# Attention blocks of a two-layer encoder: twelve copies per layer move from ScalarE to VectorE

## The chip, the cores and the metric

One core of a Trainium2 chip runs the whole program. The time is the device time of one execution, in microseconds (us), as a median of several runs. Engines are named as the profile names them: PE is TensorE, DVE is VectorE, ACT is ScalarE, POOL is GpSimd.

## The reference

Two layers, each of them (1024 tokens, width 1024):

```python
h = rms_norm(x, attn_norm[l])
x = x + hybrid_mixer(h, w_in[l], qk_gain[l], rpb[l], sink[l], out_gain[l], w_out[l])
h = rms_norm(x, ffn_norm[l])
x = x + swiglu(h, w_gu[l], w_down[l])
```

The mixer has three head groups that read the same normalised input: A, neighbourhood attention on a grid (4 heads); B, windowed attention with a sink (6 query heads on 2 key/value heads); C, dilated attention with three branches (6 heads). For every head and query block it computes

```python
p = exp(scores + bias - max)
o = (p @ v) / sum(p)
```

The head groups are normalised, joined and multiplied by `w_out`. The change touches only how `p` reaches the product `p @ v`.

## The kernel before

Each layer first makes values, queries and keys (long runs of matmuls), then does the attention, then the output projection and the feed-forward part. The attention is written out by hand as steps `k = 0` to 57 over 224 tiles, four tiles a step. A tile is one head of one block of 128 queries; its scores are 128 x 128 to 128 x 384. Steps 0 to 23 are the dilated branches. From step 24 on there are eight blocks of 128 queries with 16 tiles each, so four steps a block: tiles 0 to 3 of a block are group B (`TB` is the bias table), 4 and 5 are B too, 6 to 11 are C (`TC`), 12 to 15 are A (`TA`).

In step `k` the engines do, each in its own fixed order:

- PE (`pe_step`): the scores of the step's first pair of tiles (L2414; they wait for all four `tmin` of the step before), the scores of its second pair (they wait for the copies of the first group of the step before), the products `p @ v` of the tiles of step `k-2` (`weigh`, L2524; they wait for the copies made in step `k-1`), and then the transposes of the probabilities of step `k-1` (`half_units`, L2480).
- DVE (`dve_step`): four times `tmin` (L1682: bias table plus scores from PSUM into `T`, and the row's minimum), between them small pieces of the block's end (`finish`: denominators at L1744 to L1753, `own_heads` at L1759, `squares` at L1714, `mean` at L1720), then this engine's copies of turned probabilities (`copy_unit`, L1856), then the last piece, `finish(k, 4)`; in the first step of a block that is `own_heads`.
- ACT (`act_step`): four exponentials (L1244, each waits for its `tmin`), a result copy (L1237), one copy of turned probabilities after the third exponential, and its other copies (L1266, L1261) after the fourth.
- POOL: the weighted sum of the three branches of group C: three products (L2276, `G<-G,fac_c`) and two sums (L2288), then powers and scalings (L2234, L2241).

The turned probabilities of a step lie in one or two groups, each of them two PSUM banks: queries 0 to 63 of every chunk (first half) in one bank, queries 64 to 127 (second half) in the other. Each bank is copied by one instruction into a slot of `PT` in SBUF. A second group is there when four tiles have 12 chunks of 128 keys; then both groups hold six chunks and the copies are 128 x 384. This is so in steps 29, 32, 33, 36, 37, 40, 41, 44, 45, 48, 49 and 52, in both layers: the first step (`k` a multiple of 4) of the five blocks that begin at steps 32 to 48 and of the one at 52, and the second step (29 to 49) of six blocks. A second group of only two chunks is copied by one instruction, and its engine is as before.

Which engine makes a copy is set in one line by the copy's place `i` in the step (0 and 1 are the halves of the first group, 2 and 3 those of the second):

```python
u["engine"] = (0 if len(pt_rows) == 1 or k <= 12 or i == 1 else 1)
```

Engine 0 is DVE, 1 is ACT.

Of the kernel before, what the change touches and what calls it, by code (L numbers as in the profile page):

```python
# [22 lines left out]
def build_program(nc, x, gains, w_in, rpb, w_out, w_gu, w_down, out):  # L23
# [43 lines left out]
    with ctx:  # L67
# [241 lines left out]
        for l in range(depth):  # L309
          with ExitStack() as layer:  # L310
# [145 lines left out]
            def chunks_of(bd, s):  # L456

                k = bd["kind"]
                if k == "c3":
                    return [0]  # L460
                if k == "c2" or k in ("b0", "b7") or 6 <= s < 12:
                    return [0, 128]
                return [0, 128, 256]
# [16 lines left out]
            def first_group(b):  # L480

                return 24 + 4 * b
# [9 lines left out]
            def y_halves(fam, n, b, pair_, off):  # L492

                return dict(y=(fam, 0, n, b), items=[], engine=1, pair=pair_, off=off, half="both", group=1)
# [20 lines left out]
            def turn_of(k):  # L515

                return k if k > DILATED_STEPS else 0
# [12 lines left out]
            def by_halves(k):  # L530

                return k >= 3

            for k in range(1, GROUPS + 1):
                rows = steps[k]
                for n in range(4 * k - 4, 4 * k):
                    need = len(chunks_of(*tiles[n]))
                    if by_halves(k):
                        if not rows or len(rows[-1]["items"]) + need > 8:
                            group = len(rows) // 2  # L540
                            pair_ = TRIO[(turn_of(k) + 2) % 3] if not group else TRIO[k % 3]
                            for half in range(2):
                                rows.append(dict(y=None, items=[], engine=None, bank=pair_[half], slot=n_pt % 4, half=half,
                                                 group=group, pair=pair_))
                                n_pt += 1
                        for c in chunks_of(*tiles[n]):
                            place_of[n, c] = (rows[-2], rows[-1], len(rows[-1]["items"]))
                            for u in rows[-2:]:
                                u["items"].append((n, c))
                        continue  # L550
                    if not rows or len(rows[-1]["items"]) + need > 4:
                        pair_ = TRIO[(turn_of(k) + 2) % 3] if len(rows) < 2 else TRIO[k % 3]
                        i = max(k - 2, 0) % 2 if need == 1 else len(rows) % 2
                        rows.append(dict(y=None, items=[], engine=None, bank=pair_[i], slot=n_pt % 4, half=None, group=0))
                        n_pt += 1
                    for c in chunks_of(*tiles[n]):
                        place_of[n, c] = (rows[-1], rows[-1], len(rows[-1]["items"]))
                        rows[-1]["items"].append((n, c))
                for fam, after in (("b", 6), ("a", 7), ("c", 7)):
                    b, left = divmod(k - after - first_group(0), 4)  # L560
                    if left == 0 and 0 <= b < MT - 1:
                        used = max((u["off"] + 64 * FAM[u["y"][0]][1] if u["y"] else 64 * len(u["items"])
                                    for u in rows if u["group"]), default=0)
                        rows.append(y_halves(fam, FAM[fam][1], b, TRIO[k % 3], used))
                assert len(rows) <= 5
                second = [u for u in rows if u["group"] and u["y"] is None]
                if second and len(second[0]["items"]) <= 4:
                    first_, both_ = second
                    rows.remove(first_)
                    n_pt -= 1  # L570
                    both_.update(half="both", slot=first_["slot"])
                    for n, c in both_["items"]:
                        place_of[n, c] = (both_, both_, place_of[n, c][2])
                pt_rows = [u for u in rows if u["y"] is None]
                for i, u in enumerate(pt_rows):
                    u["engine"] = (0 if len(pt_rows) == 1 or k <= 12 or i == 1 else 1)
                order += rows
            Y_TAIL = [y_unit("b", 0, 2, MT - 1, 0, 6), y_unit("b", 2, 1, MT - 1, 1, 7), y_unit("c", 0, 3, MT - 1, 0, 6),
                      y_unit("a", 0, 2, MT - 1, 1, 7)]
# [2193 lines left out]
```

## Time and profile before

| | |
|---|---|
| median of 3 runs | 2332.53 us (2332.25 to 2333.1) |
| profiled execution, its own time | 2333.02 us |
| span of its core | 2331.3 us |
| mean granted TensorE clock | 0.998 |
| PE busy | 2280.3 us, 98% |
| DVE busy | 1617.7 us, 69% |
| ACT busy | 1056.9 us, 45% |
| POOL busy | 662.2 us, 28% |

Busy shares are means over stages with different limits. The attention blocks take about 322 to 434 us and 1480 to 1597 us of the span.

### The profile page before, as it was taken

The page shows a single profiled execution, that of the slowest core. Times are in us where ns is not written, and L with a number is a line of the kernel's source. Part 1 is how long each engine was busy: PE and PEld are TensorE (multiplying, and loading weights), DVE is VectorE, ACT ScalarE, POOL GpSimd, SP SyncE. Part 2 cuts the span into 40 slices and gives each one's busy share as a digit, 9 for nine tenths or more (in the row PEclk, how much of TensorE's full clock was granted, in tenths as well). Part 3 has the DMA queues.
Part 4 walks back from the last instruction along what each step waited for, and adds up shares of the span by engine and source line. Part 5 has one row for each costly group of instructions (what it writes and reads, how often), then busy time and mean ns, then how long its engine had stood idle before and what let it go on. Part 6 is the DMA issues. An engine that isn't in the chain of part 4 may idle for free. (4 is left out here: it accounts for less than half of the span.)

```text
span 2331.3 us, 40658 instructions
## 1 busy us (share of the span) xinstructions
PE 2280.3 (98%) x15508; PEld 1885.0 (81%) x15508; DVE 1617.7 (69%) x2921; ACT 1056.9 (45%) x2022; POOL 662.2 (28%) x571
## 2 busy tenths in 40 slices
PE   9999999999999999999999999999999999999999
PEld 9988776787888888888898887667878888888887
DVE  5389989748555555789844999896475555557898
ACT  4333689645222222443533337895452222224434
POOL 1000466312444444100010005562124444440000
PEclk9999999999999999999999999999999999999999
DMA  7231341332222211821352213313322222218223
GB/s 248 65 54 54 82 132 33 124 109 73 82 82 82 82 55 55 313 66 68 118 176 58 55 45 107 107 39 121 104 73 82 82 83 88 60 42 316 69 81 104
DMA packets 234285, 225.35 MB, mean 97 GB/s; under 512 B 50548, under 2 KB 192372, under 8 KB 234104
## 3 DMA queue, kind: packets, MB, share of 16 engines
q1 hardware_dynamic: 234104, 222.90, 30.2%
q8 instruction: 119, 1.95, 0.4%
q14 instruction: 62, 0.51, 0.1%
HBM read 171.00 MB, written 53.41 MB: 96 GB/s over the span
## 5 line engine op out<-in xcount | busy, mean ns | idle before, releaser
L1962 DVE TENSOR_TENSOR WL<-RAW,WH 128x512 fp32r<-128x512 f32 x132 | 160.4, 1216 | 151.4 <-ACT WH L1396 151.4
L2718 PE MATMUL psum<-ABH 128*128 128x512 f32 x616 | 240.1, 390 | 1.1 <-DVE X L2045 1.1
L2720 PE MATMUL psum<-ABH,ABL 128*128 128x512 f32 x616 | 239.7, 389 | 0.0
L2719 PE MATMUL psum<-ABL,ABH 128*128 128x512 f32 x616 | 239.7, 389 | 0.0
L2684 PE MATMUL psum<-HL,WH 128*128 128x512 f32 x704 | 217.4, 390 | 0.7 <-DVE HL L1968 0.7
L2684 PE MATMUL psum<-OPH_t,WH 128*128 128x512 f32 x528 | 206.0, 390 | 3.5 <-DVE U L1983 3.5
L2684 PE MATMUL psum<-OPL_t,WH 128*128 128x512 f32 x528 | 205.7, 390 | 1.0 <-DVE OPH_t L1968 1.0
L1962 DVE TENSOR_TENSOR WL<-WS,WH 128x512 fp32r<-128x512 f32 x172 | 138.4, 806 | 84.2 <-ACT WH L1396 84.2
L2316 POOL TENSOR_TENSOR WS<-RAW 128x512 f32<-128x512 f32 x84 | 143.3, 1706 | 132.0 <-DMA x_res<-X 132.0
L2348 PE MATMUL psum<-HH,UH 128*128 128x512 f32 x448 | 174.5, 389 | 0.0
L2350 PE MATMUL psum<-HH,UL 128*128 128x512 f32 x448 | 174.4, 389 | 0.0
L2349 PE MATMUL psum<-HL,UH 128*128 128x512 f32 x448 | 174.3, 389 | 0.0
L1634 DVE RECIPROCAL RM<-RM 128x512 f32<-128x512 f32 x52 | 174.0, 3346 | 0.0
L2684 PEld LDWEIGHTS psum<-HL,WH 128*128 128x128 f32 x704 | 131.7, 188 | 29.1 <-DVE HL L1968 1.5
L2209 POOL COPY QS<-QK 128x384 f32<-128x384 f32 x32 | 30.9, 965 | 435.5 <-DVE QK L1637 253.9
L2348 PE MATMUL psum<-PH,HH 128*128 128x512 f32 (+1 forms) x384 | 143.8, 374 | 0.0
L2350 PE MATMUL psum<-PH,HL 128*128 128x512 f32 (+1 forms) x384 | 142.6, 371 | 0.0
L2349 PE MATMUL psum<-PL,HH 128*128 128x512 f32 (+1 forms) x384 | 142.4, 371 | 0.0
L1244 ACT ACTIVATE T<-T,G 128x192 f32<-128x192 f32 (+3 forms) x304 | 132.1, 477 | 22.0 <-DVE G L1682 21.1
L2684 PE MATMUL psum<-OPH_b,WH 128*128 128x512 f32 x352 | 137.4, 390 | 0.0
L2718 PEld LDWEIGHTS psum<-ABH 128*128 128x128 f32 x616 | 115.6, 188 | 26.6 <-DVE X L2045 2.0
L2684 PE MATMUL psum<-OPH_t,WL 128*128 128x512 f32 x352 | 137.0, 389 | 0.0
(276 smaller groups left out, 5546.7 us busy)
## 6 DMA issues: line engine op xcount, KB each, us to landing
RAW<-in_w_gu SPq DMA_DIRECT2D x176, 256.0 KB, 3.9
WDS<-in_w_down SPq DMA_DIRECT2D x88, 256.0 KB, 2.6
UR<-in_w_in SPq DMA_DIRECT2D x56, 256.0 KB, 3.4
g_mid<-GRES SPq DMA_DIRECT2D x28, 512.0 KB, 2.6
WDK<-in_w_down SPq DMA_DIRECT2D x44, 256.0 KB, 6.3
x_res<-X SPq DMA_DIRECT2D x2, 4096.0 KB, 13.4
PR<-in_w_out SPq DMA_DIRECT2D x32, 256.0 KB, 5.1
X<-x_res SPq DMA_DIRECT2D x2, 4096.0 KB, 13.5
```

Source lines behind the costliest of these rows:

```text
L1244: a.activation(T[:, t_slot(n), off:off + w], T[:, t_slot(n), off:off + w], ACT.Exp, scale=-1.0, bias=G[:, 6 * V1 + place_:6 * V1 + place_ ...
L1634: v.reciprocal(RM[:, hf, :], RM[:, hf, :]).then_inc(rec_s, 1)
L1962: v.tensor_tensor(WL[SLOT[i, j]][:, :, :], w_source(i, j), WH[SLOT[i, j]][:, :, :].bitcast(F32), ALU.subtract).then_inc(w_lo, 1)
L2209: g.tensor_copy(dst, dilated_rows(bd, T_CQ, q, P)).then_inc(staged, 1)
L2316: g.tensor_tensor(to[i][:, :, :], first, second, op).then_inc(w_sum, 1)
L2348: t.matmul(dst, sh, mh, start=start, stop=False)
L2349: t.matmul(dst, sh, ml, start=False, stop=False)
L2350: return t.matmul(dst, sl, mh, start=False, stop=stop)
L2684: last = t.matmul(dst[:, :], w[SLOT[i, j]][:, k, :], h[o][:, k, :], start=(i in (1, 5, 6) and k == 0 and part == 0), stop=(i in (2, 3, 4) ...
L2718: t.matmul(dst, ah, bh, start=open_, stop=False, skip_group_check=True)
L2719: t.matmul(dst, ah, bl, start=False, stop=False, skip_group_check=True)
L2720: last = t.matmul(dst, al, bh, start=False, stop=shut, skip_group_check=True)
```

## The change

In steps after 12 the copies with an odd place go to DVE: 1 as before and now 3 too. So the second half of the second group goes from the end of ACT's step to DVE, right behind DVE's copy of the first group's second half and ahead of `finish(k, 4)`. PE's waits follow the engine of each copy.

```diff
                 for i, u in enumerate(pt_rows):
-                    u["engine"] = (0 if len(pt_rows) == 1 or k <= 12 or i == 1 else 1)
+                    u["engine"] = (0 if len(pt_rows) == 1 or k <= 12 or i % 2 else 1)
```

## Rows read from the trace of the kernel before

**Rows 1.** The page: span, and busy us (share) of each engine.

```profile
span 2331.3 us, 40658 instructions
PE 2280.3 (98%) x15508; PEld 1885.0 (81%) x15508; DVE 1617.7 (69%) x2921; ACT 1056.9 (45%) x2022; POOL 662.2 (28%) x571
```

**Rows 2.** Windows of two blocks: length, busy PE, PEld, DVE, ACT, POOL, clock, DMA.

```profile
354.08:370.02 15.94, 15.28 (x302) 11.07 (x303) 14.98 (x62) 14.63 (x36) 10.29 (x11) 1.00 0.14 41
370.02:385.94 15.92, 15.10 (x302) 10.99 (x300) 14.96 (x63) 14.54 (x35) 10.28 (x11) 1.00 0.14 42
```

**Rows 3.** Groups by form, 320 to 450 us: copies of 128 x 384 on either engine.

```profile
L1856 DVE COPY PT<-psum 128x384 f32<-128x384 f32 x12 | 6.6, 550 | 0.3 <-PE psum L2480 0.3
...
L1266 ACT ACTIVATE PT<-psum 128x384 f32<-128x384 f32 x36 | 16.1, 485 | 0.0
```

**Rows 4.** Waits, 320 to 430 us: total us, times, longest.

```profile
ACT T L1244 <- DVE GB L1682: 5.3, 10, 0.8
...
DVE T L1682 <- PE psum L2414: 2.8, 8, 0.4
```

**Rows 5.** Timeline of DVE, steps 40 and 41: start, us.

```profile
372.21 0.69 DVE L1753 TENSOR_TENSOR coef<-den,fac_b 128x6 f32<-128x6 f32 x1
372.83 0.54 DVE L1856 COPY PT<-psum 128x384 f32<-128x384 f32 x1
373.30 0.80 DVE L1759 TENSOR_TENSOR Y<-GB,coef 128x384 f32<-128x384 f32 x1
374.02 0.54 DVE L1682 CUSTOM_DVE_ANT_0 T<-TB,psum 128x384 f32<-128x384 f32 x1
...
374.49 0.72 DVE L1714 CUSTOM_DVE_ANT_0 junk<-Y 128x384 f32<-128x384 f32 x1
...
375.14 0.54 DVE L1682 CUSTOM_DVE_ANT_0 T<-TB,psum 128x384 f32<-128x384 f32 x1
...
376.36 0.56 DVE L1856 COPY PT<-psum 128x384 f32<-128x384 f32 x1
...
377.27 0.42 DVE L1682 CUSTOM_DVE_ANT_0 T<-TC,psum 128x256 f32<-128x256 f32 x1 [0.35 <-PE psum L2414]
```

**Rows 6.** Timeline of POOL in the same steps (windows overlap).

```profile
372.05 0.84 POOL L2276 TENSOR_TENSOR G<-G,fac_c 128x390 f32<-128x390 f32 x1 [3.60 <-ACT fac_c L1254]
...
372.85 1.95 POOL L2276 TENSOR_TENSOR G<-G,fac_c 128x390 f32<-128x390 f32 x2
...
373.64 1.15 POOL L2276 TENSOR_TENSOR G<-G,fac_c 128x390 f32<-128x390 f32 x1
...
374.87 1.22 POOL L2288 TENSOR_TENSOR G<-G 128x390 f32<-128x390 f32 x1
...
376.17 1.01 POOL L2288 TENSOR_TENSOR G<-G 128x390 f32<-128x390 f32 x1
```

**Rows 7.** Timeline of PE, steps 40 to 43, in two windows.

```profile
371.57 0.97 PE L2480 MATMUL psum<-ident,T 64*128 64x64 f32 x24
...
376.51 0.69 PE L2414 MATMUL psum<-QK 64*128 64x256 f32 x4
...
365.86 0.92 PE L2414 MATMUL psum<-QK 64*128 64x384 f32 x4 [0.32 <-DVE PT L1856]
```

**Rows 8.** Timeline of ACT, steps 40 and 41.

```profile
373.63 0.86 ACT L1266 ACTIVATE PT<-psum 128x384 f32<-128x384 f32 x2
374.60 0.62 ACT L1244 ACTIVATE T<-T,GB 128x384 f32<-128x384 f32 x1
375.73 0.62 ACT L1244 ACTIVATE T<-T,GB 128x384 f32<-128x384 f32 x1 [0.51 <-DVE GB L1682]
```

**Rows 9.** Timeline of DVE and POOL, steps 52 and 53.

```profile
421.09 0.55 DVE L1759 TENSOR_TENSOR Y<-GB,coef 128x384 f32<-128x384 f32 x1
...
421.12 2.32 POOL L2276 TENSOR_TENSOR G<-G,fac_c 128x390 f32<-128x390 f32 x2
...
421.56 0.41 DVE L1682 CUSTOM_DVE_ANT_0 T<-TB,psum 128x256 f32<-128x256 f32 x1
...
424.34 0.69 DVE L1856 COPY PT<-psum 128x512 f32<-128x512 f32 x1 [0.63 <-PE psum L2480]
```

## The prediction, as put on record before the kernel ran

> **What bounds the kernel now.** I read the page first. PE is busy 98% of the span and DVE only 69% [rows 1], which would make a longer DVE program harmless; but these are means over stages, and the change lies in one stage. So I cut that stage into its blocks with the windows view. A block of four steps takes 15.9 us, of which PE is busy 15.1 to 15.3, DVE 15.0 and ACT 14.5 to 14.6 [rows 2]. All three look full, so the busy shares can't choose between them, and I asked the view of waits and the timeline which one is late. Within a block ACT's exponentials stand idle for `tmin` on DVE: 5.3 us in 10 waits for the B tiles alone [rows 4]. In the steps that change, the first exponential of step 41 starts at 374.60, just behind its `tmin`, and the next comes 0.51 us late for the same reason [rows 5, 8]. PE in turn starts the second pair of scores of a block's last step on DVE's copy [rows 7]. DVE itself waits for PE in few places; in the two steps that matter here it does once, 0.35 us ahead of 377.27, for scores (2.8 us in 8 such waits over seven blocks [rows 4]). So DVE's own order of instructions sets the pace through the first two steps of a block, and what is added there is paid unless it falls into that one gap.
>
> **What is removed.** Twelve copies a layer, 24 in all, leave ACT. A copy takes 0.485 us [rows 3], but two in a row take 0.86 us together [rows 8], so one gives back 0.86 - 0.49 = 0.37 us. It stood behind the step's last exponential. The next thing on ACT is the exponential of the next step, and that waits for DVE [rows 8]: at a block's first step ACT only waits 0.37 us longer. At a block's second step ACT's following exponentials do come earlier, but PE's next scores there wait for DVE's copy [rows 7]. I value the removal at nothing. Its cover is DVE's lateness; if that were gone, it would be worth 24 x 0.37 = 8.9 us.
>
> **What is added, second step of a block (29 to 49).** DVE gets a copy of 128 x 384, 0.55 us as a row [rows 3]; from its start to the next instruction's it is 373.30 - 372.83 = 0.47 us [rows 5]. It goes in at the gap. From the copy at 376.36 to the next `tmin` at 377.27 there are 0.91 us, because PE can begin the scores only after the fourth `tmin` (its row starts at 376.51 [rows 7]). Two copies take 0.94 to 0.96. So I charge 0.05 us, six times a layer. From below it is 0.03; from above it is the full 0.47, if the copy has to wait for the second group's transposes, which run just ahead of those scores.
>
> **What is added, first step of a block (32 to 48).** Here there is no gap. DVE runs copy 372.83, `own_heads` (L1759) 373.30, `tmin` 374.02 [rows 5]. The second group's transposes are done at about 371.57 + 0.97 = 372.54 [rows 7], so the new copy doesn't wait. It starts at 373.30 and sends `own_heads` to 373.77. Simply added, that is 0.47 us.
>
> But L1759 takes 0.80 us here and 0.55 at step 52 [rows 5, 9], and L1753, six elements wide, takes 0.69 and ends with POOL's first product (372.05 + 0.84 = 372.89, at 372.83 DVE goes on) [rows 5, 6]. Both read two operands from SBUF, as POOL's products do. L1759's extra 0.25 fits a wait until 373.55, which is 0.70 after POOL's second product began at 372.85. In return POOL's third product takes 1.15 instead of 0.84: the two engines take turns, a whole instruction each. So *when* `own_heads` arrives matters, and the copy moves it past a turn:
>
> 1. POOL's third product starts at 373.64 [rows 6], now ahead of `own_heads` (373.77). It runs alone, 0.84, and lets go after 0.70, at 374.34.
> 2. `own_heads` runs 374.34 to 374.89; the next `tmin` starts 0.08 before that end, as it does now (373.30 + 0.80 = 374.10 against 374.02), at 374.81. It stood at 374.02: 0.79 late.
> 3. `squares` (L1714) is issued 0.47 later, at 375.28. POOL's first sum (L2288) can't start before `own_heads` lets go at 374.81; alone it takes 1.01 [rows 6], so it ends at 375.82 and lets go 0.14 earlier (0.84 - 0.70), at 375.68.
> 4. `squares` runs 0.55 from there (0.72 today, with 0.17 of waiting), and the next `tmin` starts at 375.68 + 0.55 - 0.08 = 376.15. It stood at 375.14: 1.01 late.
>
> After that DVE has no instruction with two SBUF operands until the next step. I charge 1.0 us, five times a layer. The bounds: 0.05 if the added copy fills the time in which `own_heads` and `squares` wait for POOL today (0.47 - 0.25 - 0.17); 1.0 from above, by the steps just listed.
>
 By that rule the added copy costs more than its own length here, 1.0 us a block as against 0.47 simply added; the rows above agree with it, and the sum doesn't need it.
>
> **What is added, step 52.** Here POOL runs 0.4 us later against DVE: `own_heads` starts at 421.09, just ahead of POOL's second product at 421.12 [rows 9]. With the copy in front it comes at 421.56, waits until 421.12 + 0.70 = 421.82, and the next `tmin` starts at 421.82 + 0.55 - 0.08 = 422.29 instead of 421.56: 0.73 late. Step 53 ends with 0.63 us of idle time in front of DVE's copy, where DVE waits for PE [rows 9]; PE's work there doesn't depend on these `tmin`. That leaves 0.10.
>
> **What moves.** The waits in front of PE's products and transposes now name DVE's copy instead of ACT's last one. In step 40 ACT's last copy ends at 373.63 + 0.86 = 374.49, DVE's new one at about 373.85: earlier, but nobody waited for it. No DMA, no instruction of PE or POOL is added.
>
> **The sum.** Per layer 5 x 1.0 + 6 x 0.05 + 0.10 = 5.4 us; two layers 10.8 us. Delays of one block are not made good in the next, since PE's last step of a block starts on DVE's copy [rows 7]. The profiled execution's own time is 2333.0, 0.5 above the median of the runs: 2343.8 against it, 2343.3 against the median.
>
> **Rivals.**
>
> - *Simply added* (0.47 a block, no lost turn). For it: POOL's spans are rough, and I infer the turns from four durations. Against: L1759 and L1714 are long exactly where POOL is running. Per layer 5 x 0.47 + 0.3 + 0 = 2.65, two layers 5.3: 2337.8.
> - *Absorbed*: the copy fills today's waits for POOL, because DVE gets in whenever it comes. 0.05 a block, 2 x (0.25 + 0.3) = 1.1 us: 2333.6. Against it speaks that L1753 waits 0.5 us for POOL with nothing ahead of it on DVE.
> - *ACT was late* (the other side). If the exponentials of these steps set the pace, taking 0.37 us off ACT 24 times gives -8.9 us: 2323.6. It decides only if the exponentials at a step's start run well behind their `tmin`; the first ones of step 41 start at once [rows 5, 8]. They are late only in a block's third step, where PE waits for DVE.
> - *No gap in the second step*: the new copy waits for its transposes, or these are late themselves. Up to 0.42 more, 12 times, 5.0 us on top: 2348.3.
>
> **How the numbers follow.** Lost turns 0.50, simply added 0.20, absorbed 0.10, no gap 0.08, ACT late 0.07, no change for a reason I don't see 0.05. What a measurement of this kernel can tell from no change is about 0.2%, 4.7 us, so the line lies at 2337.2. Simply added sits just above it; I count three quarters of it as slower. Slower: 0.50 + 0.08 + 0.15 + a little of the unseen = 0.75; same: 0.10 + 0.05 + most of the unseen, 0.18; faster 0.07. The time is that of the lost turns, 2343.3. The range goes down past the simple sum to 2335.5 and up to the missing gap, 2348.5; below it stay the absorbed and the ACT case. The forecast's own range is 2340 to 2346.
>
> **What would show it.** In the profile after: 24 more copies of 128 x 384 on DVE and 24 fewer on ACT; in the block's first step L1759 longer than now, near 1.1 us (374.89 - 373.77), L1714 near 0.95 (376.23 - 375.28), and POOL's third product back at 0.84; from copy to second `tmin` of the next step 3.3 us instead of 2.3; in the second step no idle time ahead of the `tmin` that waits for PE today; a block longer by about 1.05 us. I am wrong if L1759 falls to 0.55 (simply added, or absorbed if `tmin` moves by less than 0.1), or if blocks keep their length while DVE is fuller.

## The result, and the profile after

The changed kernel is slower by about a quarter of a per cent: 2339.45 us (median of 8 runs, 2337.68 to 2342.63) against 2333.47 us (8 runs, 2330.68 to 2335.75), ratio 1.0025, 95% interval 1.0016 to 1.0034, which is 3.7 to 7.9 us. The median rose by 6.0 us. The forecast's direction was right. Its time, 2343.3, was 3.9 us too long: inside the outer range of 2335.5 to 2348.5, just below the 2340 that the prediction calls its own lower end. Its rise, 10.8 us, was 4.8 us too large and lies outside the interval; the time looks 0.9 us better because the kernel before has a median of 2333.47 in 8 runs and had 2332.53 in the 3 that the forecast started from.

From the page of the kernel after, the two lines that stand in [rows 1]:

```profile
span 2337.9 us, 40658 instructions
PE 2282.0 (98%) x15508; PEld 1884.6 (81%) x15508; DVE 1630.8 (70%) x2945; ACT 1047.9 (45%) x1998; POOL 660.5 (28%) x571
```

24 instructions have gone from ACT to DVE, as intended. DVE's busy time grew by 13.1 us. That 24 copies of 0.545 us come to the same is a coincidence: by the view of lines the 128 x 384 copies grew by 11.1 us (13.2 to 24.3), `own_heads` by 3.9 (11.5 to 15.4) and `squares` of that width by 1.8 (18.0 to 19.8), while others shrank. Part of the growth is waiting inside rows that have no more work. To see this, read the same two steps as in [rows 5]. DVE's timeline of steps 40 and 41 in the kernel after (start, us; the step begins 2.09 us later on this clock than before):

```profile
374.31 0.69 DVE L1753 TENSOR_TENSOR coef<-den,fac_b 128x6 f32<-128x6 f32 x1
374.92 1.01 DVE L1856 COPY PT<-psum 128x384 f32<-128x384 f32 x2
375.86 1.13 DVE L1759 TENSOR_TENSOR Y<-GB,coef 128x384 f32<-128x384 f32 x1
376.91 0.54 DVE L1682 CUSTOM_DVE_ANT_0 T<-TB,psum 128x384 f32<-128x384 f32 x1
...
377.38 0.90 DVE L1714 CUSTOM_DVE_ANT_0 junk<-Y 128x384 f32<-128x384 f32 x1
...
378.22 0.54 DVE L1682 CUSTOM_DVE_ANT_0 T<-TB,psum 128x384 f32<-128x384 f32 x1
...
379.44 1.01 DVE L1856 COPY PT<-psum 128x384 f32<-128x384 f32 x2
380.37 0.40 DVE L1682 CUSTOM_DVE_ANT_0 T<-TC,psum 128x256 f32<-128x256 f32 x1
...
381.19 0.15 DVE L1736 TENSOR_TENSOR shift_b<-nmin,GB 128x6 f32<-128x6 f32 x1
```

And POOL's timeline there, to be held against [rows 6]:

```profile
374.14 2.43 POOL L2276 TENSOR_TENSOR G<-G,fac_c 128x390 f32<-128x390 f32 x3 [3.61 <-ACT fac_c L1254]
376.65 2.50 POOL L2288 TENSOR_TENSOR G<-G 128x390 f32<-128x390 f32 x2
```

The reader sees three things. `own_heads` (L1759) took 0.80 us and takes 1.13; `squares` (L1714) took 0.72 and takes 0.90. Neither has more work. POOL's three products take 2.43 us together, where their first and last rows before spanned 373.64 + 1.15 - 372.05 = 2.74: the third no longer gives way. And the idle time ahead of the `tmin` of step 42, 0.35 us before [rows 5], is gone.

A second view is the distance from one step's first `tmin` to the next one's. In the first two steps of the blocks from 32 to 48 it repeats to 0.01 or 0.02 us, in both layers; the third and fourth step differ from block to block, alike in both kernels. So it measures far better than the whole time does (differences of starts, each good to 0.01 us):

| | step 40 | 41 | 42 | 43 | 52 | 53 |
|---|---|---|---|---|---|---|
| before | 4.01 | 3.25 | 4.35 | 4.32 | 3.09 | 4.55 |
| after | 4.81 | 3.46 | 4.19 | 4.32 | 3.83 | 3.62 |

From the first `tmin` of step 32 to that of step 52 (five blocks) the kernel before takes 418.47 - 338.31 = 80.15 us (the hundredths by the exact starts). These are the same two rows in the kernel after, 84.36 us apart:

```profile
338.73 0.55 DVE L1682 CUSTOM_DVE_ANT_0 T<-TB,psum 128x384 f32<-128x384 f32 x1 [0.33 <-PE psum L2414]
...
423.09 0.41 DVE L1682 CUSTOM_DVE_ANT_0 T<-TB,psum 128x256 f32<-128x256 f32 x1
```

From step 28 to step 55 it is 108.2 before and 112.2 after in the first layer (322.19 to 430.39, and 322.60 to 434.82), 4.0 us more. In the second layer the stretch of five blocks is again 80.14 and 84.34, but from step 28 to step 55 it is 109.0 and 112.2, only 3.2 us more: in this execution of the kernel before, step 28 took 5.23 instead of 4.41 us, with DVE standing 0.7 us at L1769 for a DMA.

### The profile page after: what moved, and what is told of

Its sections match the earlier page's. It is cut to its first block and busy times, and to the rows that moved or that the text cites. A ratio compares the mean times of both kernels' runs of the same rounds, so it can differ in the third digit from the quotient of the medians.

```text
span 2337.9 us, 40658 instructions
## 1 busy us (share of the span) xinstructions
PE 2282.0 (98%) x15508; PEld 1884.6 (81%) x15508; DVE 1630.8 (70%) x2945; ACT 1047.9 (45%) x1998; POOL 660.5 (28%) x571
## 5 line engine op out<-in xcount | busy, mean ns | idle before, releaser
L2684 PE MATMUL psum<-OPH_b,WL 128*128 128x512 f32 x352 | 137.0, 389 | 0.0
## 6 DMA issues: line engine op xcount, KB each, us to landing
X<-x_res SPq DMA_DIRECT2D x2, 4096.0 KB, 13.2
```

The costliest lines, as they stand in the source:

```text
L2684: last = t.matmul(dst[:, :], w[SLOT[i, j]][:, k, :], h[o][:, k, :], start=(i in (1, 5, 6) and k == 0 and part == 0), stop=(i in (2, 3, 4) ...
```

## The experiments

All are read by that stretch of five blocks in the first layer, and by the whole time against runs of the kernel before on the same chip. An interval that holds 1 shows no change of the whole.

| kernel | stretch, us | whole, ratio (95% interval) |
|---|---|---|
| before | 80.15 | 1 |
| after | 84.36 | 1.0025 (1.0016 to 1.0034) |
| first_only | 84.31 | 1.0025 (1.0013 to 1.0036) |
| second_only | 80.19 | 0.9993 (0.9983 to 1.0002) |
| copy_behind | 84.95 | 1.0037 (1.0023 to 1.0052) |
| act_light | 80.17 | 1.0005 (0.9994 to 1.0015) |
| pool_light_before | 78.28 | 0.9958 (0.9943 to 0.9973) |
| pool_light_after | 78.31 | 0.9963 (0.9949 to 0.9976) |
| early_dve | 81.81 | 1.0006 (0.9997 to 1.0015) |
| early_both | 81.81 | 1.0004 (0.9995 to 1.0013) |
| late_factors | 82.11 | 1.0017 (1.0008 to 1.0026) |
| late_factors_after | 82.87 | 1.0019 (1.0010 to 1.0028) |
| coef_early | 79.23 | 0.9988 (0.9979 to 0.9997) |
| coef_early_after | 80.44 | 0.9989 (0.9980 to 0.9998) |

**1. Which of the copies cost: first_only and second_only.** Each does half of the change.

```diff
-  u["engine"] = (0 if len(pt_rows) == 1 or k <= 12 or i == 1 else 1)
+  u["engine"] = (0 if len(pt_rows) == 1 or k <= 12 or i == 1 or (i == 3 and k % 4 == 0) else 1)
```

(second_only has `k % 4 == 1`.)

> Only the copies in a block's first step (32 to 52) go to DVE; those of the second steps stay on ACT. My theory (DVE's own order sets the pace there, and the added copy makes own_heads and squares lose their turn to POOL): from the first tmin of step 32 to that of step 52 the kernel before takes 80.15 us and the changed one 84.36; this one nearly all of that, 5 x 0.82 = 4.1 us more than before, 84.2, and about 7.5 to 8 us in the whole program. The rival that both places cost alike (12 copies each): 82.2, and 3 us in all.

> Only the copies in a block's second step (29 to 49) go to DVE. My theory: they fall into the time in which DVE waits for PE's scores, 0.03 us each, so 80.3 us from step 32 to step 52 and no change that can be measured in the whole (below 1 us). The rival that every added copy is paid (0.47): 82.5 us and 5.6 us in the whole.

84.31 and 80.19 us: 4.16 of the 4.21 us belong to the five copies in the blocks' first steps, 0.04 to the five in the second steps. The same instruction costs 0.83 us at one place and 0.01 at the other (in second_only it lengthens step 41 from 3.25 to 3.28 us, and step 42 gives most of that back).

**2. Is ACT late anywhere here: act_light.** The engine map of the kernel before; ACT's copy of a second group's second half moves 8 columns and leaves out the other 376, so the results for those queries are wrong. In ACT's `copy_unit`:

```diff
-  w = pt_width(u)
+  w = 8 if u["group"] and u["half"] == 1 else pt_width(u)
```

> The kernel before with all copies where they were, but ACT's copy of the second half of a second group moves only 8 columns instead of 384 (this work is left out, so the attention of these queries is computed from stale weights). It takes most of the 0.37 us per copy off ACT and adds nothing to DVE. My theory (nobody waits for ACT there): 80.15 us from step 32 to step 52, unchanged within 0.1, and in the whole under 1 us, at most some tenths in step 53. The rival that ACT was late: 5 us or more less in the whole.

80.17 us and a ratio around 1. Taking this work off ACT is worth nothing, also in step 53 (4.55 as before). The case "ACT was late" is out.

**3. The copy behind own_heads: copy_behind.** If only the copy's own length counted, its place among DVE's instructions would not matter much.

```diff
                     for u in steps[k]:
-                        if u["engine"] == 0:
+                        if u["engine"] == 0 and not (u["group"] and k % 4 == 0):
                             copy_unit(u)
 ...
                     finish(k, 4)
+                    for u in steps[k]:
+                        if u["engine"] == 0 and u["group"] and k % 4 == 0:
+                            copy_unit(u)
```

> As the changed kernel, but in a block's first step the new copy stands behind own_heads instead of ahead of it. Simply added (0.47 a block, no turns): own_heads back at 0.80 us, its delay to POOL is gone, and from step 32 to step 52 82.6 us. Turns with POOL: own_heads is back at 0.80, but now squares (L1714), issued 0.47 later at 374.96 on the clock of the kernel before, comes after POOL's first sum has begun at 374.87; it waits until 375.75 and takes near 1.3 us instead of 0.72, so the next tmin is 1.07 late, 0.15 is won back where L1736 no longer waits for POOL, and the stretch takes 80.15 + 5 x 0.95 = 84.9 us: no better than the changed kernel.

84.95 us, against 84.9 for the turns and 82.6 for simple addition. DVE's timeline of steps 40 and 41 in this kernel:

```profile
375.58 0.55 DVE L1856 COPY PT<-psum 128x384 f32<-128x384 f32 x1
376.05 0.80 DVE L1759 TENSOR_TENSOR Y<-GB,coef 128x384 f32<-128x384 f32 x1
376.77 0.55 DVE L1856 COPY PT<-psum 128x384 f32<-128x384 f32 x1
377.24 0.54 DVE L1682 CUSTOM_DVE_ANT_0 T<-TB,psum 128x384 f32<-128x384 f32 x1
...
377.71 1.35 DVE L1714 CUSTOM_DVE_ANT_0 junk<-Y 128x384 f32<-128x384 f32 x1
```

`own_heads` is back at 0.80, and `squares`, issued at 377.71 after POOL's first sum began at 377.62, takes 1.35 us instead of 0.72. The lost turn has moved by one instruction. POOL's row:

```profile
377.62 1.02 POOL L2291 TENSOR_TENSOR G<-G 128x390 f32<-128x390 f32 x1
```

**4. The same two kernels with almost no work on POOL: pool_light_before, pool_light_after.** In both, POOL's products and sums work on 8 columns; the merging of group C's branches is left out but for these, so the results are wrong, while the order and the waits stay:

```diff
-  g.tensor_tensor(GC[:, 0, 0:6 * V1], GC[:, 0, 0:6 * V1], GC[:, i, 0:6 * V1], ALU.add)
+  g.tensor_tensor(GC[:, 0, 0:8], GC[:, 0, 0:8], GC[:, i, 0:8], ALU.add)
```

(and the products alike).

> The kernel before, with POOL's three products (L2276) and two sums (L2288) on 8 columns instead of 390: the merging of group C's branches is left out but for these, the order and the semaphores are as before. It is the reference for the same edit on the changed kernel. Turns with POOL: L1753 falls from 0.69 to near 0.16, L1759 from 0.80 to 0.55 and L1714 from 0.72 to 0.55, and the stretch from step 32 to step 52 shrinks, at most by 5 x 0.95, less where PE's scores or ACT then set the pace: 76 to 79.5 us instead of 80.15. If those long rows had another cause, 80.15.

> The changed kernel with the same light POOL (8 columns in its products and sums; the merging of the branches is left out). Compared with the one before it. Turns with POOL: without them an added copy costs its own 0.47 in a block's first step and 0.03 in the second, so the stretch from step 32 to step 52 is 5 x 0.5 = 2.5 us longer than in the light kernel before, not 4.2, and less still if PE sets the pace there. The rival that the extra came from something else than POOL: 4.2 longer, as with full POOL work.

78.28 and 78.31 us. The direction was as expected, the size was not: I had left 2.5 us for the copies themselves, and nothing is left. DVE's timeline of the light kernel before shows why:

```profile
371.23 0.21 DVE L1753 TENSOR_TENSOR coef<-den,fac_b 128x6 f32<-128x6 f32 x1
371.37 0.55 DVE L1856 COPY PT<-psum 128x384 f32<-128x384 f32 x1
371.84 0.54 DVE L1759 TENSOR_TENSOR Y<-GB,coef 128x384 f32<-128x384 f32 x1
...
375.16 0.56 DVE L1856 COPY PT<-psum 128x384 f32<-128x384 f32 x1 [0.53 <-PE psum L2480]
```

Without POOL in the way L1753 takes 0.21 instead of 0.69 and L1759 0.54 instead of 0.80, and DVE then stands idle 0.53 us before its next copy, waiting for PE. A further copy of 0.47 fits in there: with the added copies step 40 grows from 3.33 to 3.73 us and step 41 shrinks from 3.68 to 3.32. So DVE sets the pace in these steps only because it waits for POOL; the copy's own 0.47 is paid for the same reason.

**5. An attempt to use DVE's wait: early_dve and early_both.** DVE stands still in L1753, so its copy could go first.

```diff
+  if j == 3 and k >= 32 and k % 4 == 0:
+      for u in steps[k]:
+          if u["engine"] == 0:
+              copy_unit(u)
   finish(k, j)
```

(and for `k >= 32` these units are left out of the loop behind; early_both also puts ACT's first copy ahead of its result copy.)

> The kernel before, but in the first step of a block DVE's copy (place 1) stands ahead of L1753, which waits for POOL's first product there, instead of behind it; no copy changes its engine. DVE then uses the 0.5 us in which it stands still. own_heads comes at about 372.83 on the clock of the kernel before, at the same moment as POOL's second product (372.85). DVE's next tmin could start 0.67 earlier, but PE's second pair of scores waits for ACT's copy too, which ends at 373.23 against DVE's 373.37, and PE's scores, products and transposes are one chain up to the gap of 0.35 in the second step; so 0.14 a block, 79.4 us from step 32 to step 52, and 1 to 2 us in the whole. If DVE alone set the pace through both steps: 0.5 or more a block, 77.5, and 5 us.

> As early_dve, and ACT's first copy of that step stands ahead of its result copy (L1237) too. Both copies of the first group then end at about 372.8 to 372.9 on the clock of the kernel before instead of 373.37, and PE's second pair of scores follows its first at about 373.0 to 373.1 instead of 373.52. So 0.4 a block, 78 us from step 32 to step 52, and 4 to 5 us less than the kernel before in the whole, 2329. If something else holds that step: no more than early_dve.

Both expectations missed: 81.81 us, slower than before, not faster. DVE's and POOL's timelines of step 40 in early_dve:

```profile
373.78 0.56 DVE L1856 COPY PT<-psum 128x384 f32<-128x384 f32 x1
374.25 0.21 DVE L1753 TENSOR_TENSOR coef<-den,fac_b 128x6 f32<-128x6 f32 x1
374.49 1.16 DVE L1759 TENSOR_TENSOR Y<-GB,coef 128x384 f32<-128x384 f32 x1
375.57 0.54 DVE L1682 CUSTOM_DVE_ANT_0 T<-TB,psum 128x384 f32<-128x384 f32 x1
```

```profile
373.60 2.75 POOL L2280 TENSOR_TENSOR G<-G,fac_c 128x390 f32<-128x390 f32 x3 [3.60 <-ACT fac_c L1254]
...
374.40 0.84 POOL L2280 TENSOR_TENSOR G<-G,fac_c 128x390 f32<-128x390 f32 x1
```

I had put `own_heads` at "the same moment" as POOL's second product. L1753 still costs 0.21 and a link of 0.03 behind the copy, so it came at 374.49; the product had begun at 374.40 (the second row is a narrower view of the same three products). Late by 0.09 us, it waited out the whole product: 1.16 us, and the copy's gain was gone (step 40: 4.01, as before). In the whole the 1.7 us a layer don't show clear of noise. In blocks 32 and 36, where the copy itself starts 0.18 later after the step's first `tmin` (340.63 - 338.23 = 2.40 us against 373.78 - 371.56 = 2.22), L1753 lost a turn too (0.82 us) and the step took 4.81. ACT's place made no difference.

**6. Start POOL later: late_factors, late_factors_after.** In a block's first step:

```diff
-  if j == 1 and r == 0 and b > 0:
+  if j == 1 and r == 0 and b > 0 and k == GROUPS:
       branch_factors(b - 1)
 ...
   for u in mine[:1]:
       copy_unit(u)
+  if r == 0 and b > 0 and k < GROUPS:
+      branch_factors(b - 1)
```

> The kernel before, no copy moved; only ACT's small exponential fac_c, which starts POOL's three products, stands behind ACT's copy of the third tile's place instead of ahead of its third exponential, in a block's first step. POOL then starts at about 373.3 to 373.4 instead of 372.05 on the clock of the kernel before. Turns: L1753 finds no product running (0.16 instead of 0.69), own_heads comes at 372.8, ahead of POOL (0.55 instead of 0.80), squares waits some 0.3 for POOL's first product; DVE is 0.7 earlier, and PE's chain then sets the pace, as with the light POOL: 78.3 to 79 us from step 32 to step 52 instead of 80.15, and 3 to 5 us less in the whole. If POOL's sums are then too late for the block's third step, or turns are no matter: 80 us or more.

> The changed kernel (place 3 on DVE) with the same later start of POOL. Turns: own_heads comes at about 373.24, still just ahead of POOL's first product at 373.35, so the added copy makes nobody lose a turn; it costs 0.47 at most, and less where PE sets the pace: within 1 us of late_factors from step 32 to step 52 (78.5 to 79.8), instead of the 4.2 between the two kernels of the study. If the copy's cost in the changed kernel has nothing to do with where POOL stands: 4 us more than late_factors.

82.11 and 82.87 us. The first two steps did what was expected (7.04 us together instead of 7.26; with the added copies 6.99, so there the copies are free), but the third took 4.97 and 5.12 instead of 4.35. The row of DVE's timeline in step 42 of late_factors, and POOL's:

```profile
379.54 0.92 DVE L1733 TENSOR_TENSOR nmin<-GB,GAINS 128x6 f32<-128x6 f32 x1
```

```profile
378.32 2.11 POOL L2290 TENSOR_TENSOR G<-G 128x390 f32<-128x390 f32 x2
...
379.42 1.02 POOL L2290 TENSOR_TENSOR G<-G 128x390 f32<-128x390 f32 x1
```

An instruction on six elements, issued 0.12 us behind the start of POOL's second sum, waits for its end. (Line numbers are two higher in these kernels; it is L1731 of the kernel before, 0.16 us there.) In late_factors_after the next such instruction of that step waits:

```profile
379.76 0.77 DVE L1738 TENSOR_TENSOR shift_b<-nmin,GB 128x6 f32<-128x6 f32 x1
```

The two kernels differ by 0.76 us instead of 4.21, the part of the expectation that held; the 0.76 is the third steps' 0.15 us, five times.

**7. Move L1753 instead: coef_early, coef_early_after.** The four small instructions that end in L1753 each stand one tile earlier, the first of them at the end of the step before:

```diff
+  if r == 3 and 0 <= b < MT and j == 4:
+      own_sum(b, 0)
 ...
-  own_sum(b, j)
+  if j < 3:
+      own_sum(b, j + 1)
```

> The kernel before, no copy moved, POOL's start as before; DVE's four small instructions that end in L1753 each stand one tile earlier (the first at the end of the step before), so that L1753 is issued at 371.68 on the clock of the kernel before, ahead of POOL's first product (372.05), instead of behind it at 372.21. Turns: L1753 0.16 instead of 0.69; the copy starts at 372.24, own_heads at 372.71, just ahead of POOL's second product (372.85): 0.55 to 0.6 instead of 0.80; DVE is then ahead of PE, and PE's chain sets the pace as with the light POOL: step 40 takes 3.3 to 3.4 instead of 4.01, the stretch from step 32 to step 52 78.3 to 79 us, and the whole 3 to 5 us less than the kernel before. If another wait for POOL appears in the third step, as in late_factors, 80 or more.

> The same early L1753 with the changed kernel's copies. Turns: copies at 372.24 and 372.75, own_heads at 373.22, behind POOL's second product but ahead of its third, as in the kernel before: it waits until 373.55, and the next tmin starts at 374.02. So the whole lateness of the changed kernel is gone: step 40 back at 4.0 and 80.2 to 80.5 us from step 32 to step 52, the time of the kernel before. If the added copy has a price of its own beside the turns, its five times 0.47 show up on top: 82.6.

Step 40 takes 3.33 us in coef_early and 4.01 in coef_early_after, as expected. DVE's timeline of coef_early:

```profile
372.90 0.16 DVE L1753 TENSOR_TENSOR coef<-den,fac_b 128x6 f32<-128x6 f32 x1
...
373.45 0.55 DVE L1859 COPY PT<-psum 128x384 f32<-128x384 f32 x1
373.92 0.61 DVE L1759 TENSOR_TENSOR Y<-GB,coef 128x384 f32<-128x384 f32 x1
374.58 0.55 DVE L1682 CUSTOM_DVE_ANT_0 T<-TB,psum 128x384 f32<-128x384 f32 x1
```

The stretch is 79.23, not the 78.3 to 79 expected: blocks 32 and 36 gained nothing (step 32 still 4.01). There the copy starts 0.2 us later after the step's first `tmin` (341.90 - 339.50 = 2.40 against 373.45 - 371.25 = 2.20), and `own_heads` comes at 342.37, behind POOL's product, which began at 342.33:

```profile
341.90 0.56 DVE L1859 COPY PT<-psum 128x384 f32<-128x384 f32 x1
342.37 1.22 DVE L1759 TENSOR_TENSOR Y<-GB,coef 128x384 f32<-128x384 f32 x1
```

```profile
342.33 0.84 POOL L2279 TENSOR_TENSOR G<-G,fac_c 128x390 f32<-128x390 f32 x1
```

In the whole coef_early is 0.12% faster than the kernel before (0.03% to 0.21%), which is less than the 3 to 5 us expected. coef_early_after, which carries the change of this study, came out as expected: it is no slower than the kernel before, 80.44 against 80.15 us in the stretch and 0.9989 in the whole. An edit that moves no copy gives back 3.92 of the 4.21 us. The change still has a price beside that edit: 80.44 against the 79.23 of coef_early, 1.21 us where it was 4.21.

## Why the prediction was right, and what was mis-sized

**What bounds the stage.** DVE's order of instructions sets the pace in a block's first two steps: held. The reason was deeper than the text had it: DVE is late there through its waits for POOL (pool_light_before: 0.53 us of idle time in front of PE appears as they go), not through its own work.

**What is removed is worth nothing.** Held (act_light). ACT's busy time fell by 9.0 us (1056.9 to 1047.9), as the 8.9 forecast, and nobody waited for it.

**First step, 1.0 us a block by lost turns.** Held almost to the row. Step by step as forecast: `own_heads` 374.89 - 373.77 = 1.12, measured 1.13; the next `tmin` 0.79 late, measured 4.81 - 4.01 = 0.80; POOL's third product back to 0.84, measured with the other two 2.43 (0.80 + 0.80 + 0.84); `squares` 0.95, measured 0.90; the `tmin` behind it 1.01 late, measured 0.98 (378.22 - 375.14 less the 2.09 or 2.10 between the two clocks). The Trainium skill (SBUF — State Buffer, "Who interferes with whom") states a lock for a whole instruction between VectorE with two SBUF inputs and GpSimd reading SBUF; 1.13, 0.90, 1.35, 1.16 and 0.92 us for instructions that need 0.55, 0.55, 0.55, 0.55 and 0.16 alone agree with it, and so do the PSUM copies that run beside POOL in their usual 0.55. The page exempts a VectorE instruction with one SBUF input only outside the two-port modes, a condition that the prediction's sentence on it leaves out. Nor is the lock held for the whole row everywhere: DVE goes on about 0.14 us before the end of a product's or a sum's row, and POOL's scaling (L2241, 1.25 us) holds DVE only in its first 0.45 us, as the next paragraphs show. There the measurement decides. That the waits are for POOL is shown by the light kernels; that they are for this port, and why L2241 holds DVE so briefly, no run here shows.

**Second step, 0.05.** Held: 0.02 (380.37 - 379.44 = 0.93 from the first of the two copies to the next `tmin`, against 377.27 - 376.36 = 0.91 with one), 0.03 in second_only's step 41, of which 0.01 a block is left over the five blocks.

**The term that failed** is what follows the second step. "After that DVE has no instruction with two SBUF operands until the next step. I charge 1.0 us" stopped the count there, and "Delays of one block are not made good in the next" took the rest as lost. But the third step has one, L1736, and in the kernel before its row is 0.30 us long, 0.15 more than its work. There it is issued 0.29 us into POOL's scaling:

```profile
378.10 0.30 DVE L1736 TENSOR_TENSOR shift_b<-nmin,GB 128x6 f32<-128x6 f32 x1
```

```profile
377.81 1.25 POOL L2241 TENSOR_SCALAR Y<-Y,grstd 128x384 f32<-128x384 f32 x1
```

In the kernel after it comes at 381.19, when POOL is done, and takes 0.15:

```profile
379.78 1.25 POOL L2241 TENSOR_SCALAR Y<-Y,grstd 128x384 f32<-128x384 f32 x1
```

The waits end about 0.45 us into that row and not at its end: also in step 54 of the kernel before, where L1736 comes 0.09 us into it (426.80 against 426.71) and takes 0.51; and L1789, with two SBUF operands, runs in its usual 0.41 beside the rest of the row (from 378.40). The lateness falls from 1.01 to 0.85. The block costs 0.84 us, not 1.05 (388.88 - 372.11 = 16.77 us from its first `tmin` to the next block's, against 385.94 - 370.01 = 15.93).

**Step 52, 0.10.** The first part held: 0.74 late against 0.73 forecast (3.83 - 3.09). Of that only 0.03 is left at the copy of step 53, not 0.10: it starts 428.99 - 423.09 = 5.90 us after the first `tmin` of step 52, against 424.34 - 418.47 = 5.87. Then L1867, two SBUF operands again, waits for POOL's second sum and took 1.02 instead of 1.24, because it comes later against it. Steps 52 and 53 together are 7.45 instead of 7.64: -0.19 instead of +0.10.

**The sum.** 5 x 0.84 - 0.19 = 4.0 us a layer, which is what steps 28 to 55 of the first layer show, where the forecast had 5.4; 8.0 us for both instead of 10.8. The median moved by 6.0, and the interval reaches to 7.9. Of the two profiled executions the spans differ by 6.6 us: 4.0 in the first layer, 3.2 in the second, where step 28 of the kernel before stood for a DMA, and -0.6 outside. The remainder of the medians isn't settled: in the 14 profiled executions the time outside the two stretches from step 28 to step 55 lies anywhere between 2110.7 and 2118.0 us (span less the two stretches), without any order by kernel, so 2 us of a median are within that scatter; and coef_early_after, within 0.3 us of the kernel before in the stretch, came out 0.11% faster in the whole, which I can't explain either.

**The rivals.** The whole time could not choose: simply added forecast 5.3 us, nearer to the measured 6.0 than the 10.8 of the lost turns. That the time fell into the range is in part luck; the rows are what bears the lost turns out. Simply added (0.47 a block) is out by copy_behind and by step 40's 0.80. Absorbed is out by the same rows. No gap in the second step is out by second_only.

## What to carry to other kernels

Before adding an instruction to DVE, look at what POOL runs beside it, and at which DVE instructions behind the added one read two operands from SBUF: their issue times against POOL's starts decide between no cost and a whole POOL instruction. An instruction on six elements that takes 0.69 us is not noise but the place to look; here moving it 0.5 us forward gave back most of what the copies had cost. Where a stage repeats, the distance between two marks of its timeline shows hundredths of a microsecond; the whole time doesn't show one.

## What the runs showed of the hardware that I had not expected

The switch is sharp. An issue 0.09 us (374.49 against 374.40) or 0.04 us (342.37 against 342.33) behind POOL's start cost the rest of the whole product, 0.61 and 0.67 us on top of the instruction's 0.55; an issue 0.03 us ahead (421.09 against 421.12 [rows 9]) cost nothing. So 0.2 us of delay somewhere upstream, as in the blocks at 32 and 36, decides over 0.7 us in a step.

And what POOL does matters, not only when: its products and sums held DVE until about 0.14 us before their rows' end, its scaling (L2241) only for the first 0.45 of 1.25 us.
